# Second block's first mixer: index products inside the projection of queries and keys, conv projected ahead of values, first scores inside the projection of values

## The reference, cut to what matters

```python
def _sparse_attn_conv_mixer(h, rope_quarter, w_in, conv_w, w_out):
    proj = h @ w_in
    q, k, v, q_idx, k_idx, w_idx, gate_b, gate_c, x_in = jnp.split(proj, offsets, axis=-1)
    q, k = partial rope of both, 8 heads of 64
    q_idx = partial rope, 16 heads of 64;  k_idx = partial rope, one head of 64
    w_idx = w_idx * (16 ** -0.5 * 64 ** -0.5)
    attn = _dsa_attention(q, k, v, q_idx, k_idx, w_idx)
    conv = gate_b * short_conv(gate_c * x_in, conv_w)      # 3 taps, causal, per channel
    return jnp.concatenate([attn, conv], axis=-1) @ w_out

def _dsa_attention(...):      # per query
    score = sum over 16 heads of relu(q_idx . k_idx) * w_idx, causal
    sel = the 64 keys with the largest score
    out = softmax(q . k / 8 over sel) @ v, for each of 8 heads
```

## Time and profile before

| what | value |
|---|---|
| median of 3 runs | 1088.29 us (1087.21 to 1093.13) |
| the profiled execution's own time | 1089.14 us |
| its span | 1087.3 us |
| mean granted clock of PE | 0.991 |
| busy PE / PEld / DVE / ACT / POOL | 1044.9 / 872.4 / 655.1 / 564.1 / 99.8 us |
| chain that ended last, PE's share | 82% |
| high part of a 128x2048 unit with gain, on ACT (L572, two instructions) | 2.2 us |
| high part of one without gain | 1.9 us |

### The profile page before, as it was taken

The page is one execution under the profiler, slowest core; times in us unless marked ns, Lnnn a source line. Parts: engine busy times, 40 slices in busy tenths (PEclk is TensorE's granted clock), DMA queues, the critical chain, the costliest instruction groups (busy, mean ns, idle before and its releaser), DMA issues.

```text
span 1087.3 us, 13860 instructions
## 1 busy us (share of the span) xinstructions
PE 1044.9 (96%) x5080; PEld 872.4 (80%) x5080; DVE 655.1 (60%) x1020; ACT 564.1 (52%) x855; POOL 99.8 (9%) x127
## 2 busy tenths in 40 slices
PE   7999999999999999999979999999997999999997
PEld 6887878887888887878867888888886878888886
DVE  5575665456565555647876755545654867555453
ACT  6566455437454455644544744454454647445541
POOL 2010110001000001104440100000140001000000
PEclk9999999999999999999989999999999999999999
DMA  8746136215545545633422655554252225555521
GB/s 336 279 174 230 58 117 219 110 58 183 204 159 190 215 149 187 237 136 118 152 75 103 234 188 196 188 192 153 70 190 105 78 92 221 191 195 190 193 78 39
DMA packets 28462, 176.31 MB, mean 162 GB/s; under 512 B 3248, under 2 KB 3392, under 8 KB 9984
## 3 DMA queue, kind: packets, MB, share of 16 engines
q1 hardware_dynamic: 26784, 170.08, 43.2%
q0 software_dynamic: 1456, 5.48, 1.4%
q10 hardware_dynamic: 176, 0.13, 0.0%
HBM read 174.62 MB, written 1.05 MB: 162 GB/s over the span
## 4 chain that ended last, share of the span: by engine, by line
PE 82%; DVE 9%; ACT 3%; issue 3%; POOL 2%; DMA 1%; SPq 0%; DVEq 0%; ACTq 0%; POOLq 0%
PE PS L1468 71%; PE PS L1537 3%; DVE w_lo L983 3%; PE PS L1589 2%; PE PS L1572 2%; ACT w_hi L572 2%; PE PS L1679 2%; DVE w_lo L981 1%; DMA x<-in_x 1%; DVE work L1127 1%; POOL h L487 1%; PE PS L1580 1%; DVE h L1347 1%; POOL arena L480 1%; ACT work L653 0%
## 5 line engine op out<-in xcount | busy, mean ns | idle before, releaser
L983 DVE SCALAR_TENSOR_TENSOR w_lo<-w_raw,gcol,w_hi 128x512 fp32r<-128x512 f32 (+4 forms) x322 | 269.4, 895 | 208.4 <-ACT w_hi L572 207.8
L572 ACT ACTIVATE w_hi<-w_raw,gcol 128x512 fp32r<-128x512 f32 (+4 forms) x322 | 243.4, 824 | 99.4 <-PE PS L1468 98.5
L1468 PE MATMUL PS<-w_hi,hT_hi 128*128 128x512 f32 (+3 forms) x904 | 246.4, 393 | 7.8 <-DVE hT_lo L998 3.0
L1468 PE MATMUL PS<-w_hi,hT_lo 128*128 128x512 f32 (+3 forms) x904 | 240.2, 386 | 0.0
L1468 PE MATMUL PS<-w_lo,hT_hi 128*128 128x512 f32 (+3 forms) x904 | 238.9, 385 | 0.9 <-DVE w_lo L983 0.8
L1468 PEld LDWEIGHTS PS<-w_lo,hT_hi 128*128 128x128 f32 x904 | 167.5, 188 | 35.9 <-DVE w_lo L983 2.4
L1468 PEld LDWEIGHTS PS<-w_hi,hT_hi 128*128 128x128 f32 x904 | 164.0, 189 | 40.1 <-issue 3.8
L1468 PEld LDWEIGHTS PS<-w_hi,hT_lo 128*128 128x128 f32 x904 | 168.1, 189 | 33.2
L981 DVE TENSOR_TENSOR w_lo<-w_raw,w_hi 128x2048 fp32r<-128x2048 f32 (+1 forms) x70 | 135.7, 1954 | 83.7 <-ACT w_hi L572 83.6
L572 ACT ACTIVATE w_hi<-w_raw 128x2048 fp32r<-128x2048 f32 (+1 forms) x70 | 114.6, 1644 | 106.7 <-PE PS L1468 106.7
L1468 PE MATMUL PS<-w_hi,gT_hi 128*128 128x512 f32 x408 | 113.9, 392 | 0.0
(11 more groups left out here) (151 smaller groups left out, 786.0 us busy)
## 6 DMA issues: line engine op xcount, KB each, us to landing
w_raw<-in_w SPq DMA_DIRECT2D x64, 1024.0 KB, 4.8
w_raw<-in_w_gu SPq DMA_DIRECT2D x22, 1024.0 KB, 4.8
w_raw<-in_w_in SPq DMA_DIRECT2D x11, 1024.0 KB, 7.6
w_raw<-in_w_dn SPq DMA_DIRECT2D x22, 512.0 KB, 5.4
w_raw<-in_w_mem_k SPq DMA_DIRECT2D x4, 1024.0 KB, 4.9
w_raw<-in_w_out SPq DMA_DIRECT2D x4, 1024.0 KB, 4.8
w_raw<-in_w_cq SPq DMA_DIRECT2D x4, 1024.0 KB, 4.7
w_raw<-in_w_mem_v SPq DMA_DIRECT2D x4, 1024.0 KB, 4.8
```

Source lines behind the costliest of these rows:

```text
L572: ins = act.activation(w_hi[:, u % RING, k * w:(k + 1) * w], w_raw[:, u % RAW, k * w:(k + 1) * w], ACT.Copy, scale=1.0 if col is None else ...
L983: ins = dve.scalar_tensor_tensor(out=lo, in0=raw, scalar=gcol[:, col + TURNED * k:col + TURNED * k + 1], in1=hi, op0=ALU.mult, op1=ALU.sub ...
L1468: mm = pe.matmul(bank(t, j)[:, 0:width], rows[:, kc0 + k, tok], w[:, s, at:at + width], start=begin and i == 0, stop=end and i == 2)
```

## The change

- The index rows are turned at hook (0, 2) of `qk`, and the index blocks stand at its hooks (1, 0) to (1, 3), three at each, in an order that mixes the tiles (`INDEX_ORDER`). Each of the twelve has its own home in SBUF (`INDEX_HOME`), so the waits for reuse (`idx_used`) go.
- ACT's and DVE's orders are written anew around them: DVE's index sums and rounds stand between low parts of the next projection's units, ACT alone copies the turned queries and keys.
- `conv` is projected before `v_gate`. Queries and keys are turned inside `conv`; conv's input inside `v_gate`, and also the scores of heads 0 and 1.
- The gate is turned inside the attention, into banks 0 and 1, and copied by ACT; POOL waits for that only with the last multiply. POOL, not DVE, makes conv's low part.
- The out projection runs (0,0), (0,1), (1,0), (0,2), (0,3), (1,1), (1,2), (1,3), with the attention rows' turn at (1,0) and the stream's at (1,3).
- Two fewer ring banks are used, so the later attention (`mla`) swaps its pairs of banks.

```diff
@@ schedule and DMA order
-            ("qk", ...), ("v_gate", ...), ("conv", ...),
+            ("qk", ...), ("conv", ...), ("v_gate", ...),
@@ constants
+        mla.score_bank, mla.prob_bank = 6, 4
+        INDEX_ORDER = [4, 0, 5, 1, 6, 2, 7, 3, 8, 9, 10, 11]
+        INDEX_HOME = [work[:, k, :] for k in range(6)] + [region(6144 + 512 * k, 512) for k in range(4)] + [region(4096 + 512 * k, 512) for k in range(2)]
@@ POOL, index_sum and convolve
-                    if b == 0:
-                        pool.wait_ge(idx_used[0], 1)
-                    weighed.then_inc(idx_used[1], 1)
-                    pool.wait_ge(idx_used[1], b + 1)
+                    steps.link(pool.tensor_tensor(idx_part, rel, w, ALU.mult))
+                pool.wait_ge(gate_copied, TT)
                 pool.tensor_tensor(y_conv, y_conv, gbT, ALU.mult).then_inc(conv_ready, 1)
+                for c in range(4):
+                    pool.wait_ge(conv_high, c + 1)
+                    pool.tensor_tensor(hT_lo[:, 4 + c, :], y_conv[:, c, :], hT_hi[:, 4 + c, :].bitcast(F32), ALU.subtract).then_inc(conv_low, 1)
@@ ACT
-            group(4, rows2(qk_tok), even_rows, index_turned)
-            index_relu(0, 8)
-            group(4, rows2(vg_tok), even_rows, lambda: index_relu(8, 12))
-            act.wait_ge(padded, 4)
-            group(4, rows2(cx_tok), even_rows, lambda: plain_banks(4, turned_qk3), 1)
-            plain_banks(4, in_turn(paired(gbT), paired(uT)))
-            attention(dsa)
+            split_to(n["used"] + 3)
+            n["used"] += 4
+            index_turned()
+            evict(0, rows2(qk_tok), even_rows)
+            for i in range(4):
+                index_relu(3 * i, 3 * i + 3)
+                if i < 3:
+                    split_to(n["used"] + i)
+            evict(1, rows2(qk_tok), even_rows)
+            split_to(n["used"] + 3)
+            n["used"] += 4
+            evict(0, rows2(cx_tok), even_rows)
+            split_to(n["used"])
+            act.wait_ge(padded, 4)
+            act.wait_ge(idx_complete, 1)
+            plain_banks(4, turned_qk3, None)
+            split_to(n["used"] + 2)
+            evict(1, rows2(cx_tok), even_rows)
+            split_to(n["used"] + 3)
+            n["used"] += 4
+            plain_banks(2, paired(uT))
+            evict(0, rows2(vg_tok), even_rows)
+            split_to(n["used"])
+            attention(dsa, [0])
+            split_to(n["used"] + 1)
+            attention(dsa, [1])
+            evict(1, rows2(vg_tok), even_rows)
+            attention(dsa, range(2, 5), False)
+            for t in range(TT):
+                act.wait_ge(gate_turned, t + 1)
+                act.activation(gbT[:, :, token_cols(t)], PS[:, t, :]..., ACT.Copy).then_inc(gate_copied, 1)
+            attention(dsa, range(5, dsa.H), False)
@@ DVE (index_sum now takes one block)
-            after_group(4)
+            after_group(4, ahead=2)
             rotate(heads_of(qi_tok, 64), 0, 8, cos3, sin3).then_inc(h_ready, 1)
-            after_group(1)
+            after_group(1, ahead=2)
...
-            after_group(4, index_turned)
-            rotate(heads_of(qk_tok, 64), 0, 8, cos3, sin3).then_inc(h_ready, 1)
-            index_sum()
+            split_to(n["used"] + 3)
+            n["used"] += 4
+            plain_banks(4, tiles2(qiT), 0)
+            index_sum(0)
+            split_to(n["used"])
+            index_sum(1)
+            index_sum(2)
+            split_to(n["used"] + 1)
+            index_sum(3)
             steps.link(dve.tensor_tensor(score[:, 0:P], score[:, 0:P], causal[:, P:2 * P], ALU.add))
+            split_to(n["used"] + 2)
             largest(0)
-            after_group(4)
+            split_to(n["used"] + 3)
+            dve.wait_ge(acc_copied, n["copied"])
+            rotate(heads_of(qk_tok, 64), 0, 8, cos3, sin3).then_inc(h_ready, 1)
+            n["used"] += 4
             dve.wait_ge(idx_complete, 1)
             steps.link(dve.tensor_tensor(score[:, P:3 * P], score[:, P:3 * P], causal[:], ALU.add))
-            largest(1)
+            largest(1, range(0, 5))
+            split_to(n["used"])
+            largest(1, range(5, TOP_K // 8))
...
+            split_to(n["used"] + 2)
+            dve.wait_ge(acc_copied, n["copied"])
             for t in range(TT):
                 dve.tensor_tensor(cx_tok[:, t, 0:512], cx_tok[:, t, 0:512], cx_tok[:, t, 512:1024], ALU.mult).then_inc(h_ready, 1)
+            split_to(n["used"] + 3)
+            n["used"] += 4
+            plain_banks(2, paired(uT))
+            split_to(n["used"])
+            attention(dsa, [0])
+            split_to(n["used"] + 1)
+            attention(dsa, range(1, dsa.H + 2), False)
-            for c in range(4):
-                dve.wait_ge(conv_high, c + 1)
-                dve.tensor_tensor(hT_lo[:, 4 + c, :], ..., ALU.subtract).then_inc(conv_low, 1)
@@ PE
+            def first_index():
+                turned(5)
+                index_products(0, 3)
+            project(4, 2, wide, copies=2, hooks={(0, 2): after_h(turn_index, 2), (1, 0): first_index, (1, 1): lambda: index_products(3, 6),
+                                                 (1, 2): lambda: index_products(6, 9), (1, 3): lambda: index_products(9, 12)})
             project(4, 2, wide, copies=2, hooks={(1, 1): after_h(lambda: turn_rows(qk_tok, False))})
-            turn_parts((vg_tok, 512))
-            turn_half(cx_tok, 0)
-            turned(4)
-            attention(dsa)
+            project(4, 2, wide, copies=2, hooks={(0, 2): lambda: turn_half(cx_tok, 0), (1, 2): first_heads, (1, 3): lambda: attention(dsa, [1])})
+            attention(dsa, [2])
+            copied()
+            attention(dsa, [3])
+            for t in range(TT):
+                for b in range(4):
+                    mm = pe.transpose(PS[:, t, P * b:P * (b + 1)], vg_tok[:, t, 512 + P * b:512 + P * (b + 1)], ident[:])
+                mm.then_inc(gate_turned, 1)
+            attention(dsa, range(4, dsa.H + 3))
...
-            project(4, 2, wide, kc0=4, chunks=KC, hooks={(0, 2): attention_rows, (1, 2): tile0})
+            project(4, 2, wide, kc0=4, chunks=KC, hooks={(1, 0): attention_rows, (1, 3): tile0},
+                    order=[(0, 0), (0, 1), (1, 0), (0, 2), (0, 3), (1, 1), (1, 2), (1, 3)])
```

91 lines of the change are left out of this document (38 added, 53 removed).

## The result

The changed kernel takes 1094.19 us (median of 15 runs, 1092.68 to 1096.61), the kernel before on the same chip 1089.53 (15 runs). The ratio is 1.0041, 95% interval 1.003 to 1.0052: 4.7 us slower, which is inside the half per cent named as no change, though the interval reaches just past it. The prediction had 1089.6 and a whole range of 1080.5 to 1094.5; it had the change itself at +1.3 us. The measured time lies above the forecast's own range, 1084 to 1093, and at the upper end of the whole one.

The account below looks back on a forecast made before the run. PE bounds the kernel, busy 1044.9 of 1087.3 us. From 1089.14: -1.8 + 2.3 + 5.3 to T, -6.3 behind, +1.9 in the out projection gives 1090.4, or 1089.6 against the median; own range 1084 to 1093, whole 1080.5 to 1094.5.

Parts of the forecast that it names:

- The early turn removes its wait: At the index rows' turn, PE's 1.47 us wait for ACT goes, since ACT stands ready there.
- rival 4: The index rows' second rotation is late, so their turn still waits: +1.5 us on any case; no chance of its own.
- DVE and GpSimd hold each other in the index stage: DVE's sums and low parts lengthen beside GpSimd's sum; PE waits 5.3 us in conv's fourth unit, bounds 0 and 7.
- Rival 1: DVE and GpSimd disturb each other little in the index stage: no low-part wait, no clock fall, 1080.8 us; chance 0.25.
- T: The end of the last projection (values and gate): 544.77 us in the kernel before, forecast 550.6.
- Rival 3: DVE and GpSimd fully exclude each other in the index stage: wait 8 us, time 1092.5; chance 0.06.
- The restart at T + 5.2: PE goes on in attention 5.2 us after the last projection, behind tile 1's eviction; bounds 2.9 and 7.4.
- S: The start of the out projection: 572.41 us in the kernel before, forecast 571.9.
- Rival 2: The low clock lasts through attention after the late restart: +6.3 us instead of +2.0, time 1093.9; chance 0.11.
- Conv's low parts on GpSimd: Ahead of the out projection, conv's first high part 0.35 us and four low parts on GpSimd 3.3 us.
- The out projection: The new product order makes PE wait 1.9 us at the turn of the stream's tile 1; bounds 0 and 2.7.
- The later layer: The later attention's swapped banks cost nothing, as the same waits cover them.

Follow-up runs that it names:

- the filler: The changed kernel with 36 unused identity turns put into PE's 4.24 us wait ahead of attention's fourth head; 1091.47 us, ratio 1.0022.
- the run with both copies on ACT: The changed kernel with old out order, DVE in order of need, out projection's second low part behind two maxima, gate turned first, ACT copying both conv-row banks; 1082.97 us.
- two edits more: On the kernel with the three edits: ACT copies both banks of turned conv rows, and attention's rows are turned ahead of the out projection's second product; 1080.79 us, ratio 0.9902.
- the kernel with the three edits: The changed kernel with old out order, DVE's queue in order of need, and out projection's second low part behind two maxima with the gate turned first; 1083.07 us.

## Why the prediction was right, and where its sizes were off

Step by step, from the traces:

- *The early turn removes its wait.* Right: PE goes from the index rows' turn into the next product at once (467.77 to 469.44, no wait over 0.2), and the prediction's rival 4 didn't come about.
- *DVE and GpSimd hold each other in the index stage.* Right in place, cause and size: the fourth low part was forecast for 512.4 and is ready at 511.6, the wait 5.3 and 5.01. The run without GpSimd's sum shows the cause. Rival 1 (they don't disturb each other), which had 0.25, is what that run builds: no wait on the low part, but 1085.8 instead of its 1080.8, as the restart still comes 5.4 us behind T where rival 1 had 3.6, with low clock behind it. Rival 3 (full exclusion) was right in kind, as the single instructions show, and wrong in its price, a wait of 8.
- *The price of that wait.* The step that failed first: it was entered as 5.3 us and no more, while the prediction priced the clock only for the restart. Products of 2.07 and 1.57 us behind it (1.07 at full clock) are 1.5 us that had no term. Forecast from the start to T +5.8, measured +6.6.
- *The restart at T + 5.2.* Measured T + 5.4, released as forecast by the eviction of tile 1. From there the last exp ended 14.0 us later and not 12.4. Two things make the 1.6 us. The clock was priced at 2.0 and costs 3.0, by the filler, which takes it away. And the seventh head's bias on DVE took 1.37 us instead of 0.17 beside GpSimd's last product of the convolution, for which there was no term; PE waits 0.61 us there, in the filler's run too. With the conv rows' way S came 22.6 us behind T and not 21.3: -5.0 instead of -6.3. Rival 2 was the clock's mechanism at 6.3; the truth lay between.
- *Conv's low parts on GpSimd.* ACT 1.32 and four in 2.78 us; PE waits 0.97 for the last of them. From the last exp to S it is 3.2 us, forecast 3.7.
- *The out projection.* Forecast +1.9, measured +1.8.
- *The later layer.* Forecast nothing; 1.4 us come from low clock behind the same wait of 3.33 us (the rows of 829.56 and 831.41, against 1.17 in the kernel before). It is the clock's share, not a step of the change: from that turn to the later layer's first scores it is 18.9 us in the changed kernel and 17.5 in the kernel before, but 17.6 in the run with both copies on ACT, which has the same swapped banks, and 17.7 in the kernel before with the new out order. Among the runs none to two such products stand there.

Of the 3.4 us between the forecast +1.3 and the measured +4.7, the low clock makes 1.5 + 1.0 + 1.4 = 3.9, the held bias 0.6 and the restart 0.2, less what came out shorter than forecast: 0.3 at the wait for the low part, 0.4 on the rest of the way to T, 0.5 on the conv rows' way, 0.1 in the out projection, together 3.4. The mechanism and its places were right; what was mis-sized above all is one term, what a gap costs beyond its own length.

Some of it is luck. The prediction put "slower by over half a per cent" above 1093.7 us, from a median before of 1088.29 in 3 runs; the changed kernel takes 1094.19, and only because the kernel before came out at 1089.53 in 15 runs is the change still within half a per cent. The sum's terms as printed also give 1090.5, not 1090.4, and +1.4 for the change.

## What to carry to other kernels

Work pulled forward under another stage is paid from the queue of the engine that serves it there: write out that engine's queue with the times at which each result is needed, and order it by need before taking the sum for a loss; here the order alone was worth 4.5 us, and the same change with ordered queues and the old out order became a gain of 0.5%, of 1% with two edits more. Price a gap of several us on PE as its length plus the work behind it at low clock: 1.5 us behind 5.01 here, 3.0 behind 4.24, and behind the same 4.24 only 1.7 in the run without GpSimd's sum, so the price is a range and not a number. Price a step that DVE and GpSimd do at the same time by the disturbed durations of both. When two edits draw on one slack (T and the restart), their gains don't add. And compare kernels that ran on different chips by their ratios to one that ran on each.

## What the runs showed of the hardware that was not expected

- The hold between DVE and GpSimd goes both ways, and it takes instructions with one input too. GpSimd's tap took 4.27 us beside DVE's low parts, 1.90 alone; DVE's comparison of 128x384 took 2.57 us beside GpSimd and 0.36 without; its largest-of-eight search went on at 0.28 to 0.29 beside GpSimd's additions. Of a held instruction's own duration 0.14 to 0.2 us lie beside the other's.
- The clock can fall with PE busy all the time: 0.65 in the changed kernel from 459 to 462 us, at the end of products of 80 columns, with PE busy for 3.00 of 3.00 us.
- One and the same wait is followed by full clock in one execution and not in the next. PE's timeline of the kernel with the three edits, at an early wait of 1.46 us:

```profile
138.99 2.05 PE L1507 MATMUL PS<-w_hi,hT_hi 128*128 128x512 f32 x4 [1.46 <-issue]
```

and of the changed kernel, at the same instruction:

```profile
137.50 1.16 PE L1509 MATMUL PS<-w_hi,hT_hi 128*128 128x512 f32 x4 [1.46 <-issue]
```

  The stage's first product stood between 431.8 and 435.2 us in the fourteen profiled executions, in code that is the same up to there. A single profile is thus no measure of 1 to 3 us; stretches within one are, where no chance of the clock lies inside them, and so are medians of one chip.
